# Score banks for the attention outputs, a second buffer of tiles for the last two experts, and context rows gathered as quarter rows

## What is computed

```
for l in range(2):
    # token mixer: windowed attention (8 heads, band of +-128, plus context) and
    # latent attention (8 heads, 64 + 32 wide keys, dense over all 1280 keys)
    p = softmax(q @ k.T)            # one softmax over latent and context keys
    o = p @ v                       # per head
    x = layer_norm(ALPHA * x + gate * merge(o_a, o_b))
    # 16 experts, each takes its top tokens: 128 latent rows, and 32 context rows in layer 0
    xg = h[top_idx]
    y  = (silu(xg @ w_gate) * (xg @ w_up)) @ w_down * top_aff
    x  = layer_norm(ALPHA * x + gate * scatter_add(y))
```

## Time and profile before

| | |
|---|---|
| time, median of 3 runs | 4216.95 us (4215.39 to 4220.05) |
| the profiled execution's own time | 4216.5 us, its span 4214.8 us |
| mean granted clock of TensorE | 0.981 |
| PE busy | 4039.2 us, 96% |
| DVE, ACT, POOL busy | 1892.8, 1076.1, 253.7 us |
| attention, layer 0 and layer 1 | about 347 to 817 us, 2592 to 3024 us |
| experts, layer 0 and layer 1 | about 1447 to 2292 us, 3509 us to the end |

### The profile page before, as it was taken

The page is one execution under the profiler, slowest core; times in us unless marked ns, Lnnn a source line. Parts: engine busy times, 40 slices in busy tenths (PEclk is TensorE's granted clock), DMA queues, the critical chain, the costliest instruction groups (busy, mean ns, idle before and its releaser), DMA issues.

```text
span 4214.8 us, 77861 instructions
## 1 busy us (share of the span) xinstructions
PE 4039.2 (96%) x31338; PEld 2856.4 (68%) x31338; DVE 1892.8 (45%) x4216; ACT 1076.1 (26%) x2469; POOL 253.7 (6%) x254
## 2 busy tenths in 40 slices
PE   8998999999999799999999999999999987999997
PEld 4555777655544588888887555777644446999996
DVE  2235666522235443333334444666533355444446
ACT  1225666400012111111111323666400120100103
POOL 0000000000000011111111000000000000101013
PEclk9999999999999899999999999999999998999998
DMA  6111000322244798888886211000222437999996
GB/s 209 55 51 50 16 16 16 118 73 70 70 156 183 268 284 267 266 267 266 266 266 203 85 63 56 16 16 16 71 45 45 156 115 233 328 330 327 330 324 223
DMA packets 568272, 655.05 MB, mean 155 GB/s; under 512 B 20404, under 2 KB 495172, under 8 KB 568088
## 3 DMA queue, kind: packets, MB, share of 16 engines
q1 hardware_dynamic: 548024, 603.17, 44.5%
q0 software_dynamic: 19488, 47.21, 4.5%
q10 hardware_dynamic: 576, 2.10, 0.1%
HBM read 581.03 MB, written 71.39 MB: 155 GB/s over the span
## 4 chain that ended last, share of the span: by engine, by line
PE 82%; DVE 3%; DMA 2%; issue 1%; DVEq 1%; ACT 1%; SPq 1%; POOL 0%; ACTq 0%; POOLq 0%
PE PS L714 34%; PE PS L1214 9%; PE PS L1243 9%; PE PS L718 8%; PE PS L886 6%; PE PS L1053 5%; PE PS L944 3%; PE PS L937 2%; PE PS L1237 1%; PE PS L857 1%; DVE arena L1617 1%; PE PS L854 1%; PE PS L729 1%; DVE arena L2061 1%; SPq L410 1%
## 5 line engine op out<-in xcount | busy, mean ns | idle before, releaser
L714 PE MATMUL PS<-arena 128*128 128x160 f32 (+4 forms) x7200 | 1773.2, 408 | 12.9 <-DVE arena L1617 5.1
L714 PEld LDWEIGHTS PS<-arena 128*128 128x128 f32 x7200 | 1143.5, 191 | 616.3 <-issue 559.0
L1617 DVE TENSOR_TENSOR arena<-arena,PS 128x256 f32<-128x256 f32 (+3 forms) x668 | 293.6, 448 | 1056.5 <-ACT arena L1586 566.8
L1617 DVE TENSOR_TENSOR arena<-arena 128x1024 f32<-128x1024 f32 (+9 forms) x826 | 590.3, 732 | 353.9 <-PE PS L714 234.1
L718 PEld LDWEIGHTS PS<-arena 128*128 128x128 f32 (+2 forms) x3218 | 379.0, 141 | 260.6 <-issue 148.0
L718 PE MATMUL PS<-arena 128*128 128x128 f32 (+2 forms) x3218 | 490.4, 280 | 45.0 <-DVE arena L1617 16.3
L1214 PE MATMUL PS<-arena 128*64 128x128 f32 x8192 | 457.2, 274 | 3.8 <-DVE arena L1617 1.7
L1214 PEld LDWEIGHTS PS<-arena 128*64 128x64 f32 x8192 | 452.6, 138 | 8.9 <-issue 3.9
L1243 PE MATMUL PS<-arena 128*64 128x256 f32 x3584 | 396.7, 382 | 1.8 <-DVE arena L1617 1.3
L1586 ACT ACTIVATE arena<-PS 128x160 f32<-128x160 f32 (+1 forms) x256 | 74.5, 291 | 1176.1 <-PE PS L714 654.3
L1243 PEld LDWEIGHTS PS<-arena 128*64 128x64 f32 x3584 | 274.3, 138 | 119.6 <-issue 12.4
(11 more groups left out here) (218 smaller groups left out, 2256.1 us busy)
## 6 DMA issues: line engine op xcount, KB each, us to landing
arena<-in_w_exp_gate SPq DMA_DIRECT2D x128, 1024.0 KB, 6.5
arena<-in_w_exp_up SPq DMA_DIRECT2D x128, 1024.0 KB, 9.0
arena<-in_w_exp_down SPq DMA_DIRECT2D x128, 1024.0 KB, 7.7
arena<-in_w_ada SPq DMA_DIRECT2D x24, 2048.0 KB, 20.5
arena<-in_w_in SPq DMA_DIRECT2D x32, 512.0 KB, 5.4
h_transposed<-arena SPq DMA_DIRECT2D x20, 512.0 KB, 4.4
x_mid<-arena SPq DMA_DIRECT2D x18, 512.0 KB, 3.5
moe_sum<-arena SPq DMA_DIRECT2D x18, 512.0 KB, 3.5
```

The lines of the kernel that those rows point to most:

```text
L714: m = pe.matmul(o, lt, rh, start=start and i == 0, stop=stop and i == n - 1)
L1617: return dve.tensor_tensor(o, x, y, op)
```

## The change

1. Attention: `outputs` writes to the middle bank of the scores of A of the next step (`out_bank`) rather than bank 6, and waits for the exponential that reads it; chunk 2 of B goes to that set's last bank (`turned`). Scores B of the next step wait for `ob` at the chunk that has that bank. Chunk 2 of W is copied by DVE, not ACT (`ON_DVE`). PE's order is now scores A (256), W chunk 0, scores A (512, 512), W chunks 1 and 2, the band scores, then all three B chunks.
2. Last two experts: tiles 4 to 7 have buffers of their own in the first two slots of the weight ring. The loads of tiles 0 to 3 are issued at f = 5 and not 3; two of their moments go behind the f loop, their scaling and gain go beside the gate and up products of expert 15, all eight biases behind `own_rows`, which no longer waits for stores; all stores come last.
3. Layer 0: the 32 context rows are gathered as 128 quarter rows of 256 floats, turned by two 128x128 transposes; the matmul and copy that turned the row indices go.

The diff, cut to its core:

```diff
-    n |= dict(sM=16 * ctx + 192, tr=24 * ctx + 288, pt_a=24 * ctx + 192, pt_d=96, kw=24)
+    n |= dict(sM=16 * ctx + 192, tr=24 * ctx + 288, pt_a=24 * ctx + 160, pt_d=128, kw=24)
...
-        xgc = at(O + 11264, D)
+        xgc = at(O + 11264, 256)
...
+        zb = at(R, 4, D)
...
-            return zq[:, n % EARLY, :]
+            return zq[:, n, :] if n < EARLY else zb[:, n - EARLY, :]
...
-        def bank(part, ci):
-
-            return 6 + ci % 2 if part == "W" else 7 - ci % 2
+        def out_bank(n):
+
+            return score_set("A", n + 1) + 1
+
+        def turned(part, n, ci, blocks):
+
+            b = 6 + ci % 2 if part == "W" else 7 - ci % 2
+            if part == "B" and ci == 2:
+                b = score_set("A", n + 1) + 2
+            return PS[:, b, 0:blocks * P]
+
+        ON_DVE = {"A": (0,), "W": (0, 2), "B": (0,)}
...
-                for n in group(0):
-                    out_rows(n)
+                sp.wait_ge(*s("au", 8 * (E - 1) + 2))
                 sp.wait_ge(*s("sc", 32 * (E - 1)))
-                sp.wait_ge(*s("out_st", 16 * EARLY))
                 for n in group(1):
                     ld(z_tile(n), z_d[(TC + n) * P:(TC + n + 1) * P, :], G[f"big{n % EARLY}"])
-                for n in group(1):
+                for n in range(SEQ // P):
...
-                        return [lambda: None, banded] if full else [context]
+                        return [banded] if full else [context]
...
+                        if i == 1 and part == "B" and later(N):
+                            pe.wait_ge(*s("ob", N))
...
+                            if part == "W" and later(N):
                                 pe.wait_ge(*s("ob", N))
-                        elif not full:
+                            if part == "B":
+                                pe.wait_ge(*s("pt_a", pa_count(l, lp, n, 1)))
+                        elif (part, ci) == ("A", 2):
+                            pe.wait_ge(*s("pt_d", pd_count(l, lp, n, 1)))
+                        elif (part, ci) == ("W", 0):
                             pe.wait_ge(*s("pt_a", pa_count(l, lp, n, 1)))
-                        elif ci == 2:
-                            pe.wait_ge(*s("pt_d", pd_count(l, lp, n, "AWB".index(part) + 1)))
-                        else:
-                            pe.wait_ge(*s("pt_a", pa_count(l, lp, n, ci + (1 if part == "W" else 3))))
+                        elif (part, ci) == ("W", 1):
+                            pe.wait_ge(*s("pt_a", pa_count(l, lp, n, 2)))
+                        elif (part, ci) == ("W", 2):
+                            pe.wait_ge(*s("pt_d", pd_count(l, lp, n, 2)))
+                        elif (part, ci) == ("B", 0):
+                            pe.wait_ge(*s("pt_a", pa_count(l, lp, n, 3)))
+                        elif (part, ci) == ("B", 1):
+                            pe.wait_ge(*s("pt_d", pd_count(l, lp, n, 3)))
+                        elif (part, ci) == ("B", 2) and ahead:
+                            pe.wait_ge(*s("pM", 2 * N + 3))
...
-                    if full:
-                        pe.wait_ge(*s("pt_d", pd_count(l, lp, n, 2)))
-                        pe.wait_ge(*s("pt_a", pa_count(l, lp, n, 5)))
-                    else:
+                    o = out_bank(n)
+                    if not full:
                         pe.wait_ge(*s("pt_a", pa_count(l, lp, n, 2)))
+                        if ahead:
+                            pe.wait_ge(*s("pM", 2 * N + 3))
...
-                    pe.wait_ge(*s("pt_a", pa_count(l, lp, n, last_copy(lp))))
+                            pe.matmul(PS[half(g), o, 0:P], v, PT[:, 20 + g * nw + i, :], start=i == 0, stop=i == nw - 1)
                     if full:
-                        pe.wait_ge(*s("pt_d", pd_count(l, lp, n, 3)))
+                        pe.wait_ge(*s("pt_d", pd_count(l, lp, n, 4)))
+                    else:
+                        pe.wait_ge(*s("pt_a", pa_count(l, lp, n, 3)))
...
+                        if kt in (4, 8):
+                            pe.wait_ge(*s("pt_a", pa_count(l, lp, n, 3 + kt // 4)))
...
-                        weave(scores(p, *nx, "A") if nx else [], transposes(p, lp, n, "W"))
-                        weave(transposes(p, lp, n, "B"), scores(p, *nx, "W") if nx else [])
-                        outputs(p, lp, n)
+                        keys = scores(p, *nx, "A") if nx else []
+                        turns = transposes(p, lp, n, "W")
+                        band = scores(p, *nx, "W") if nx else []
+                        weave(keys[:2], turns[:1])
+                        for step in keys[2:] + turns[1:] + band + transposes(p, lp, n, "B", bool(nx)):
+                            step()
+                        outputs(p, lp, n, bool(nx))
                         if nx:
-                            weave(scores(p, *nx, "B"), transposes(p, *nx, "A", (lp, n)))
+                            weave(scores(p, *nx, "B"), transposes(p, *nx, "A"))
...
-                    pe.matmul(PS[0:CAP_C, 6, 18 * E:19 * E], idcf[0:E, :], ident[0:E, 0:E], start=True, stop=True)
...
-                        for k in range(KD):
-                            m = pe.transpose(PS[:, 2, k * 32:(k + 1) * 32], xgc[0:CAP_C, k * P:(k + 1) * P], ident[0:CAP_C, 0:CAP_C])
+                        for i in range(2):
+                            m = tr(PS[:, 2, i * P:(i + 1) * P], xgc[:, i * P:(i + 1) * P])
...
+                        if full and ci in ON_DVE[part]:
...
-                        if b == 0 and f == 3:
+                        if b == 0 and f == 5:
...
-                        if b is not None and f >= 4:
-                            moments_a(group(b)[f - 4])
+                        if b == 0 and f >= 6:
+                            moments_a(f - 6)
+                        if b == 1 and f < 4:
+                            scaled_a(f)
+                        if b == 1 and f >= 4:
+                            moments_a(f)
...
-                    if b is not None:
-                        roots_a(b)
+                    if b == 1:
+                        roots_a(1)
                     if not last:
                         rows_a(e + 1)
                     elif l:
                         row_roots(0, 2)
-                    if b is not None:
-                        scaled_a(group(b)[0])
+                    if b == 0:
+                        moments_a(2)
+                    if b == 1:
+                        scaled_a(group(1)[0])
                     act.wait_ge(*s("yt", 8 * e + 2))
                     A(UU[:, 0, :], PS[:, 5, 0:256], ACT.Copy).then_inc(s["sil"], 1)
-                    if b is not None:
-                        for n in group(b)[1:]:
+                    if b == 0:
+                        moments_a(3)
+                        roots_a(0)
+                    if b == 1:
+                        for n in group(1)[1:]:
...
+                        copy_chunk(p, lp, n, "W", 2)
...
-                        m = dve.tensor_copy(icur[0:CAP_C, 1:2], idxT[0:CAP_C, 1, ds(e, 1)])
+                        m = dve.tensor_copy(icur[:, 1:2], idxC[:, ds(e, 1)])
...
-                        for n in group(b)[3:]:
-                            gain(n)
+                        roots_d(0)
...
+                        if ending(l, e) == 1 and 1 <= f < 5:
+                            gain(f - 1)
...
-                        pool.indirect_dma_start(out=xgc[0:CAP_C, :], out_offset=None, in_=x1_d,
-                                                in_offset=bass.IndirectOffsetOnAxis(ap=icur[0:CAP_C, 1:2], axis=0)).then_inc(s["gat"], 16)
+                        pool.indirect_dma_start(out=xgc, out_offset=None, in_=x1_d.rearrange("t (j n) -> (t j) n", j=4),
+                                                in_offset=bass.IndirectOffsetOnAxis(ap=icur[:, 1:2], axis=0)).then_inc(s["gat"], 16)
...
-                    pool.wait_ge(*s("out_st", 16 * EARLY))
...
+                    if ending(l, e) == 1:
+                        for n in group(0):
+                            pool.wait_ge(G[f"big{n}"], 32)
                     if not (isinstance(e, int) and e == 0):
                         scatter(e - 1)
-                    if ending(l, e) == 0:
-                        for n in group(0)[:3]:
-                            bias(n)
                     if ending(l, e) == 1:
-                        for n in group(0)[3:]:
-                            bias(n)
                         own_rows()
-                        for n in group(1):
+                        for n in range(SEQ // P):
```

55 lines of the change are left out of this document (23 added, 32 removed).

## The result

The changed kernel takes **4187.2 us** (median of 4 runs, 4184.5 to 4191.7) against 4216.2 us of the kernel before on the same chip: ratio 0.9931, 95% interval 0.9919 to 0.9943. It is 29 us faster where 43 were forecast, and 2 us above the upper end of the range. Its profiled execution took 4185.7 us, its span is 4183.7 us, 31.1 less than before.

A forecast was written before the change was run, and what follows sets the result against it. PE was taken as the bound, busy 4039.2 of 4214.8 us, plus two attention waits. Gains of 18.5 + 17.5 + 6.0 + 1.0 = 43.0 us gave 4174 us, range 4164 to 4185.

The forecast's parts named there:

- The step: Full attention step, both layers: both PE waits go, gaining 0.57 to 0.62 us per step, taken as 0.59.
- Both waits: PE's idle 0.36 us (ACT's copy of W's chunk 2) and 0.26 us (copy of B's chunk 1) per step would go.
- the 0.16 laid out: Slack in us before B's chunk 2 would wait for the next step's exponential A; the change's thinnest place.
- Rival (c): Attention: B's chunk 2 or the outputs wait for the exponential, 0.24 us of each of 62 steps stays; 4189, chance 0.11.
- Layer 0: Attention of layer 0: 32 full steps gain 18.9 us, 18.5 after the passage's loss.
- a loss of 0.4: Layer 0's passage from context to full steps: outputs wait for a full exponential ahead of all products, 0.4 us lost.
- Layer 1: Attention of layer 1: 17.5 us kept; some 2 us beyond this turns into waiting for the stream's sums.
- the forecast's own rule: Layer 1: 30 steps times the step's gain, less 0.2 us by which `masked` is later in its step.
- Quarter rows: Layer 0's experts: two full transposes replace eight 32-row ones, 0.38 us x 16 = 6.1, taken as 6.0.
- The 0.1 that I took for the gather: Layer 0, expert 0: the gather's fourfold descriptors, uncovered there, cost 0 to 1 us, taken as 0.1.
- The ending: Last two experts: 1.0 us gained of 7.5 removable, as POOL's four biases hold up DVE in expert 15.
- the bound of 4: Last two experts: the forecast's lower bound, 4 us lost; the upper was 7.5 gained.

The follow-up runs named there:

- two_more_turns: Two transposes of B's chunk 1 done twice per full step, against the changed kernel without its last-two-experts part: 4204.4 us (one run), step 13.04 us.
- rows_alone: Only the quarter rows of layer 0's context, put on the kernel before: 4208.7 us, ratio 0.9977.

## Why the prediction was wrong

- **The step: wrong in size.** The step that failed is the count of idle time ahead of the sum: "Ten transposes take 1.45, where at 0.11 each they should take 1.09: 0.36 idle", "two transposes take 0.48, where 0.22 would do: 0.26 idle", with "up to 0.05 that may be the change of tile shape". The change of shape costs 0.10 ahead of the band and 0.15 ahead of the outputs. So the waits were 0.26 and 0.11, 0.37 together, and 0.38 were measured. I had multiplied a transpose inside a run of them (0.109) by their number, but the price could be read in the trace of before. In the context steps of layer 0 two transposes stand ahead of a product of 64 rows, and no wait stands between:

```profile
368.48 0.44 PE L718 MATMUL PS<-arena 128*128 128x128 f32 x2 [0.21 <-ACT arena L1376]
368.85 0.70 PE L870 MATMUL PS<-arena 64*128 64x256 f32 x4
```

They take 368.85 - 368.48 = 0.37, which is 0.22 + 0.15. The bracket of the earlier trace rows hinted at it too: it has 0.28 us for the wait that I counted as 0.36. Over 62 steps 0.21 us each are 13 us, the size of the whole miss; by the table the errors of the other terms come to 1 us in favour together.
- **What went right of it.** Both waits went. The exponential came in time: ACT has read its sum by 2756.04, and B's chunk 2 begins near 2755.49 + 0.87 = 2756.36, so the slack is under 0.32 us; the 0.16 laid out was not measured. Rival (c), which gives nearly the measured time (4189), is not what happened, since no wait is there, as two_more_turns shows; that its time fits is chance.
- **Layer 0**: 32 x 0.38 = 12.2 us, and 15.0 measured. The rest, 2.8, lies ahead of the full steps, where I had forecast nothing and a loss of 0.4: the context steps' period went from 5.07 to 4.70 us (2.1 up to the seventh), and the passage to full steps gained 0.9.
- **Layer 1**: the chain from the last `masked` by SP to the stream held. By the forecast's own rule 30 x 0.38 - 0.2 = 11.2; 9.2 were measured, with 2.0 us turned into waiting at the place named.
- **Quarter rows**: 6.0 forecast, 4.8 alone. The term that failed is the price of the ten transposes, 0.97 + 0.22 = 1.19. It holds in the first two experts, and the first period gains 0.39; in the others they take 1.28 to 1.31 and the period gains 0.26 to 0.29. The change of shape is not the reason, for the 0.97 had it already (0.87 + 0.10); the cause of the 0.1 stays open. In the changed kernel the stage gained 6.7, because PE's gap in expert 0 went from 2.69 to 0.85 us, which I had not looked for. The 0.1 that I took for the gather at expert 0 shows in no run: from the transposes to the first expert are 4.41 us in rows_alone and 4.42 before.
- **The ending**: 1.0 forecast as gain, 3.2 lost from expert 13's down product on (the 1.4 of the table has 1.8 gained ahead of it in layer 1's experts, which differ by as much between profiles), inside the bound of 4. The mechanism was right: biases from 17.2 us after expert 15's start (16.6 forecast), DVE held by each, the tail behind ACT's first part at 34.0. The term that failed is "a gain of 1.0", and in it the time at which DVE is done. It was laid out for 37.9 us after the expert's start (4176 less 4138.1), and the last down product came at 41.8, 7.6 us later than before. DVE's wait of 4.38 us for the down weights was in none of my rows: its first weight sums began 16.8 us after the start, where they had begun at 12.6. The full clock in the last product gave 2.8 back.

The Trainium skill (SBUF — State Buffer, Who interferes with whom) has the rule that DVE's instructions with two SBUF inputs and GpSimd's that read SBUF block each other for whole instructions. The rows agree: two weight sums take 7.29 us beside two biases and 2.36 without them.

## What to carry to other kernels

Read an engine's idle time from a row where the same pair of instructions stands without a wait, not from the price of one instruction times their number; where none exists, put the difference into the range. Before an elementwise operation is moved to POOL "beside" DVE, price it on DVE itself: here it costs 1.3 us there, and 2.4 us of both engines on POOL. When code ahead of a critical stage moves, look for a wait on a load at that stage's start: 1.8 to 2.7 us went by it in expert 0. And before an edit of the last stage is credited with a gain, see what clock its last product was granted: up to 2.9 us hang on that alone.

## What the runs showed of the hardware

- From 128x128 transposes to products of 64-row tiles PE loses 0.10 us (the band) or 0.15 (the context steps), to products of 64-column tiles 0.15, and about as much back, in float32; the weight load's row shows 0.17 us of "issue" there. To products of 96-row tiles it loses nothing (four transposes 0.44).
- The last down product, 112 instructions, takes 15.13 to 15.18 us where the gap ahead of it is 2.67 or 2.73 us (granted clock 0.81 over it, 0.50 in its first 3 us, which is 1.2 GHz), 13.66 to 13.99 where it is 2.15 to 2.37 (granted clock 0.50 to 0.60 in its first 3 us), and 12.31 where it is 0.76 to 2.11. In the changed kernel the gap of 5.88 us lies 17 us ahead of the product, and by its start the clock is 1.00 again.
- Two weight sums on DVE take 2.35 us alone and 7.29 beside two POOL biases.
